# Hybrid conformer and sliding-window attention block on one Trainium2 core: value projection with features as rows, the queries' blocks in a buffer of their own, convolution taps behind each rotation

## The chip, the core and the metric

The kernel runs on one core of a Trainium2 chip. TensorE (PE in the profile, with its weight loads as PEld) multiplies, VectorE (DVE), ScalarE (ACT) and GpSimd (POOL) do the elementwise work, and SyncE (SP) issues the DMAs of the weights. The metric is device time in microseconds (us) of one execution; lower is better.

## The reference

One layer over 2048 tokens and 1024 features, in float32. Cut to what matters here:

```
u = rms_norm(h, g_pre_mix);  z = u @ w_in          # columns: GLU 2*512 | q 512 | k 128 | v 128 | gates 2*1024
a, b = split(z_glu);  c = a * sigmoid(b)
c = silu(layer_norm(causal_depthwise_conv(c, 31 taps)));  y_conv = c @ w_conv_out
q = apply_rope(q, 8 heads of 64);  k = apply_rope(k, 2 heads of 64);  v = 2 heads of 64
y_attn = sliding_window_sink_attention(q, k, v, sinks) @ w_attn_out   # chunks of 64, each sees itself and the one before
y = sig(gate_a) * y_conv + sig(gate_b) * y_attn;   h = h + rms_norm(y @ w_out)
u = rms_norm(h);  gate, val = split(u @ w_up);  gate = causal_depthwise_conv(gate, 3 taps)
h = h + rms_norm((gelu(gate) * val) @ w_down)
h = h + (p @ w_ple) * sigmoid(h @ w_ple_gate)
```

## The kernel before

**Tiling.** The 2048 tokens are worked off in four slices of T = 512 (`for c in range(CHUNKS)`). Inside a slice nearly every activation stands with its features on the 128 partitions and the 512 tokens along the row. Each float32 product is made of three: the stationary weight tile and the moving activations are split in a high and a low part (`w_hi`, `w_lo`, `u_hi`, `u_lo`), and `product` issues hi x hi, hi x lo and lo x hi. A block is eight 128 x 128 weight tiles; `full_block` runs its 24 matmuls of 512 columns into one PSUM bank. In the first slice a block arrives unsplit: ScalarE rounds it to `w_hi` (L356) and GpSimd subtracts (L318); in the others both parts are loaded.

**Order.** Each engine has its own program, written out by hand, and runs it strictly in that order; semaphores join them. In the mixing part of a slice TensorE computes the GLU blocks, then four query blocks and the key block (`B_QKV + j`, j = 0 to 4), the value block, then the attention, whose stages stand between the `gate_a` blocks, then the merge.

**Rotation.** For each of the five blocks ScalarE writes a copy with swapped halves into `rope_b` (four instructions, L409; `rope_b` has two buffers, so block j from 2 on waits until rotation j-2 is done), VectorE multiplies by cosine and sine and adds (L1101, L1102, then L1105 into `qT` for queries, or four times L1109 into `k_dup` for the keys). Every rotation counts up `rope_done`, so the keys' rotation is the fifth in a slice.

**Taps.** The 31-tap convolution is done by VectorE, one instruction for each tap and feature group (L1065 for tap 0, L1069 for the others). `early_taps(1, ...)` puts the 30 of the second half of the features ahead of the rotations: 8, 8, 8 and 6 of them ahead of rotations 0 to 3, none ahead of the keys'. Another 64 stand between the steps of the attention. After the last, VectorE sums the four groups (L1175), and TensorE turns that into a mean (`conv_mean`, L834), for which it waits in the middle of a `gate_b` block.

**Attention.** `attend_q` (ScalarE, L417 and L418) spreads two chunks' queries into the block-diagonal `q_diag`, which VectorE has zeroed (L1097). `scores(i)` is 24 small matmuls; `score_maxima` (VectorE), `attend_exp` (ScalarE), the normalisation (VectorE), a transpose (L794) and the product with the values (L802) follow. Between `scores(i)` and that transpose TensorE runs two `gate_a` blocks. `q_diag` shares its memory with part of `rope_b`, so `attend_q(0)` waits for all five rotations and for a new zeroing in every slice.

**Values.** Values are wanted with tokens on the partitions. So here the activations are the stationary side: L760 to L762 are 96 matmuls of 128 columns. ScalarE copies the bank into `v_even` and `v_odd` (L426 to L430) before the exponentials.

## Time and profile before

| what | us |
|---|---|
| median of 3 runs (lowest, highest) | 3052.93 (3051.05, 3054.32) |
| the profiled execution, its own time | 3054.54 |
| span in its trace | 3052.7 |
| PE busy | 2903.9 |
| DVE busy | 1564.0 |
| ACT busy | 920.4 |
| POOL busy | 299.7 |

The span runs from the first to the last instruction. Busy TensorE time counts overlapping matmuls once, and it says nothing about how wide they are. The chain that ended last is what set the time: at each step the work that released the next. The four slices begin at about 0, 827, 1566 and 2303 us of the span; the stretch that the change touches is about 60 to 250 us in the first and 890 to 1010 us in the second. The third and fourth have the timing of the second.

### The profile page before, as it was taken

The page shows a single profiled execution, that of the slowest core. Times are in us where ns is not written, and L with a number is a line of the kernel's source. Part 1 is how long each engine was busy: PE and PEld are TensorE (multiplying, and loading weights), DVE is VectorE, ACT ScalarE, POOL GpSimd, SP SyncE. Part 2 cuts the span into 40 slices and gives each one's busy share as a digit, 9 for nine tenths or more (in the row PEclk, how much of TensorE's full clock was granted, in tenths as well). Part 3 has the DMA queues.
Part 4 walks back from the last instruction along what each step waited for, and adds up shares of the span by engine and source line. Part 5 has one row for each costly group of instructions (what it writes and reads, how often), then busy time and mean ns, then how long its engine had stood idle before and what let it go on. Part 6 is the DMA issues. An engine that isn't in the chain of part 4 may idle for free.

```text
span 3052.7 us, 33514 instructions
## 1 busy us (share of the span) xinstructions
PE 2903.9 (95%) x13232; PEld 2401.6 (79%) x13232; DVE 1564.0 (51%) x2535; ACT 920.4 (30%) x1661; POOL 299.7 (10%) x126
## 2 busy tenths in 40 slices
PE   6888899999899999999999999999999999899998
PEld 5776778887788778888878887888887878788887
DVE  6894477325778426412458834540356862542035
ACT  3463343333426223111233522210123541311013
POOL 2223334444200000000000000000000000000000
PEclk8799999999999999999999999999999999999999
DMA  5445757877743454555454344455555345455555
GB/s 208 172 164 215 284 213 289 290 285 280 262 167 137 158 184 176 194 194 189 184 207 171 133 179 176 183 193 194 189 189 208 142 151 195 160 193 193 193 193 179
DMA packets 180925, 600.37 MB, mean 197 GB/s; under 512 B 18336, under 2 KB 37024, under 8 KB 180768
## 3 DMA queue, kind: packets, MB, share of 16 engines
q1 hardware_dynamic: 163872, 589.83, 53.0%
q10 hardware_dynamic: 16896, 8.39, 0.9%
q8 instruction: 105, 1.72, 0.2%
q14 instruction: 52, 0.43, 0.0%
HBM read 461.84 MB, written 136.31 MB: 196 GB/s over the span
## 4 chain that ended last, share of the span: by engine, by line
PE 79%; DVE 15%; ACT 3%; issue 2%; DMA 1%; POOL 0%; ACTq 0%; POOLq 0%; SPq 0%; DVEq 0%
PE ps L690 22%; PE ps L691 21%; PE ps L692 21%; DVE conv_acc L1069 7%; PE ps L711 4%; PE ps L712 4%; PE ps L715 4%; PE ps L731 1%; DVE prob L1151 1%; DVE s_max L1130 0%; POOL w_lo L318 0%; DVE ca_lo L1162 0%; DVE y_tmp L1205 0%; PE ps L724 0%; DVE h L1042 0%
## 5 line engine op out<-in xcount | busy, mean ns | idle before, releaser
L690 PE MATMUL ps<-y_hi,w_hi 128*128 128x512 f32 x1536 | 602.9, 392 | 7.8 <-POOL w_lo L318 5.2
L692 PE MATMUL ps<-y_hi,w_lo 128*128 128x512 f32 x1536 | 598.9, 390 | 0.0
L691 PE MATMUL ps<-y_lo,w_hi 128*128 128x512 f32 x1536 | 598.8, 390 | 0.0
L1069 DVE SCALAR_TENSOR_TENSOR conv_acc<-conv_in,col,conv_acc 128x512 f32<-128x512 f32 x480 | 350.9, 803 | 0.8
L318 POOL TENSOR_TENSOR w_lo<-w_stage,w_hi 128x1024 fp32r<-128x1024 f32 x122 | 299.5, 2456 | 515.5 <-ACT w_hi L356 515.5
L690 PEld LDWEIGHTS ps<-y_hi,w_hi 128*128 128x128 f32 x1536 | 289.1, 188 | 71.3 <-DVE f_val L1262 4.3
L692 PEld LDWEIGHTS ps<-y_hi,w_lo 128*128 128x128 f32 x1536 | 289.0, 188 | 60.6
L691 PEld LDWEIGHTS ps<-y_lo,w_hi 128*128 128x128 f32 x1536 | 289.2, 188 | 59.9 <-issue 1.0
L690 PE MATMUL ps<-u_hi,w_hi 128*128 128x512 f32 x800 | 320.9, 401 | 0.4 <-POOL w_lo L318 0.4
L691 PE MATMUL ps<-u_lo,w_hi 128*128 128x512 f32 x800 | 313.5, 392 | 0.0
L692 PE MATMUL ps<-u_hi,w_lo 128*128 128x512 f32 x800 | 313.4, 392 | 0.0
L690 PE MATMUL ps<-f_hi,w_hi 128*128 128x512 f32 x768 | 301.5, 393 | 2.2 <-DVE f_lo L1283 2.2
L691 PE MATMUL ps<-f_lo,w_hi 128*128 128x512 f32 x768 | 299.5, 390 | 0.0
L692 PE MATMUL ps<-f_hi,w_lo 128*128 128x512 f32 x768 | 299.5, 390 | 0.0
L356 ACT ACTIVATE w_hi<-w_stage 128x1024 fp32r<-128x1024 f32 x122 | 129.1, 1059 | 267.2 <-PE ps L692 214.4
L1293 DVE TENSOR_TENSOR f_lo<-ps,f_hi 128x512 fp32r<-128x512 f32 x8 | 5.2, 686 | 339.9 <-ACT f_hi L597 339.9
L690 PEld LDWEIGHTS ps<-u_hi,w_hi 128*128 128x128 f32 x800 | 152.0, 190 | 34.1 <-issue 3.4
L691 PEld LDWEIGHTS ps<-u_lo,w_hi 128*128 128x128 f32 x800 | 151.9, 190 | 33.5 <-issue 3.0
L692 PEld LDWEIGHTS ps<-u_hi,w_lo 128*128 128x128 f32 x800 | 151.5, 189 | 32.1
L711 PE MATMUL ps<-y_hi,w_hi 128*128 128x512 f32 x384 | 154.5, 402 | 17.8 <-ACT y_hi L548 9.9
L690 PEld LDWEIGHTS ps<-f_hi,w_hi 128*128 128x128 f32 x768 | 144.6, 188 | 33.4 <-DVE f_lo L1283 2.6
L691 PEld LDWEIGHTS ps<-f_lo,w_hi 128*128 128x128 f32 x768 | 144.5, 188 | 30.6 <-issue 1.0
(179 smaller groups left out, 3991.9 us busy)
## 6 DMA issues: line engine op xcount, KB each, us to landing
w_hi<-split_weights SPq DMA_DIRECT2D x366, 512.0 KB, 3.2
w_lo<-split_weights SPq DMA_DIRECT2D x366, 512.0 KB, 4.2
w_stage<-in_weights SPq DMA_DIRECT2D x122, 512.0 KB, 4.3
split_weights<-w_hi SPq DMA_DIRECT2D x122, 512.0 KB, 2.6
split_weights<-w_lo SPq DMA_DIRECT2D x122, 512.0 KB, 3.9
x_rows<-in_x SPq DMA_DIRECT2D x5, 2048.0 KB, 10.2
out_h<-ple ACTq DMA_DIRECT2D x32, 256.0 KB, 5.2
p_rows<-in_p SPq DMA_DIRECT2D x4, 512.0 KB, 5.9
```

The source lines that it names most:

```text
L318: nc.gpsimd.tensor_tensor(w_lo[:, b % SLOTS], w_stage[:, b % SLOTS], w_hi[:, b % SLOTS].bitcast(F32), ALU.subtract).then_inc(w_lo_ready, 1)
L356: copy(w_hi[:, b % SLOTS], w_stage[:, b % SLOTS], ACT.Copy).then_inc(w_hi_ready, 1)
L690: nc.tensor.matmul(bank, w_hi[:, slot, kk], hi, start=start, stop=False)
L691: nc.tensor.matmul(bank, w_hi[:, slot, kk], lo, start=False, stop=False)
L692: return nc.tensor.matmul(bank, w_lo[:, slot, kk], hi, start=False, stop=stop)
L711: nc.tensor.matmul(ps[:, banks[o]], w_hi[:, slot, first + o], hi[:, k], start=(k == 0), stop=False)
L712: nc.tensor.matmul(ps[:, banks[o]], w_lo[:, slot, first + o], hi[:, k], start=False, stop=False)
L715: last = nc.tensor.matmul(ps[:, banks[o]], w_hi[:, slot, first + o], lo[:, k], start=False, stop=(k == 7))
L731: nc.tensor.matmul(ps[:, BC], ones[:, :], diag[:, :, :].rearrange("p t n -> p (t n)"), start=True, stop=True).then_inc(bc_ready, 1)
L1069: V.scalar_tensor_tensor(dst, src, column("conv_w", t + j * TAPS), dst, ALU.mult, ALU.add).then_inc(conv_tap, 1)
L1151: V.tensor_tensor(prob[:, s], prob[:, s], s_rec[:, s].unsqueeze(2).broadcast_to([P, PAIRS, P]), ALU.mult).then_inc(pn_ready, 1)
L1293: V.tensor_tensor(f_lo[:, F1 - NP + k], ps[:, PV + k], f_hi[:, F1 - NP + k].bitcast(F32), ALU.subtract).then_inc(p_lo, 1)
```

## The change

It touches three engines, all in the stretch from the query blocks to the first scores.

1. The value block becomes a `full_block` like the others: 24 matmuls of 512 columns with features as rows, ScalarE copies the bank to `v_feat`, and `value_rows` on TensorE transposes it back into the same bank with four 128-column transposes. It stands behind `scores(0)`. ScalarE's copies into `v_even` and `v_odd` wait for them.
2. `q_diag` and `v_feat` get buffers of their own. `q_diag` is zeroed once, in the first slice, ahead of rotation 3.
3. ScalarE calls `attend_q(0)` ahead of the keys' swapped copies, as soon as four rotations are done; `scores(0)` waits for the fifth.
4. VectorE's early taps stand behind each rotation: 8, 8 and 8 behind rotations 0 to 2, none behind rotation 3, 6 behind the keys'.

```diff
-        q_diag = sb("q_diag", [P, 2, PAIRS, P], F32, at + 18 * K)
+        q_diag = sb("q_diag", [P, 2, PAIRS, P], F32)
+        v_feat = sb("v_feat", [P, T], F32)
...
@@ ScalarE
+                def attend_q(i):
+
+                    for s in range(2):
+                        now = ds(2 * CH * i + CH * s, CH)
+                        copy(q_diag[0:CH, s, :, 0:CH], qT[0:CH, :, now], ACT.Copy)
+                        copy(q_diag[CH:P, s, :, CH:P], qT[CH:P, :, now], ACT.Copy).then_inc(q_diag_ready, 1)
+
                 for j in range(PAIRS + 1):
                     split_block(B_QKV + j + 2)
+                    if j == PAIRS:
+                        act.wait_ge(rope_done, c * (PAIRS + 1) + PAIRS)
+                        act.wait_ge(q_zeroed, 1)
+                        attend_q(0)
                     done(B_QKV + j)
...
-                    if j >= 2:
+                    if 2 <= j < PAIRS:
                         act.wait_ge(rope_done, c * (PAIRS + 1) + j - 1)
...
-                act.wait_ge(rope_done, (c + 1) * (PAIRS + 1))
-                act.wait_ge(q_zeroed, c + 1)
-                attend_q(0)
                 split_block(B_GA + 1)
                 done(B_QKV + PAIRS + 1)
+                copy(v_feat[:, :], ps[:, V_BANK], ACT.Copy).then_inc(v_out, 1)
+                act.wait_ge(vt_done, c + 1)
                 v_new = four(ps[:, V_BANK])
@@ TensorE
-                ready(B_QKV + PAIRS + 1)
-                v_slot = (c * NB + B_QKV + PAIRS + 1) % SLOTS
-                for t in range(TT):
...
-                last.then_inc(block_done, 1)
+                full_block(B_QKV + PAIRS + 1, V_BANK, u_hi, u_lo)
                 pe.wait_ge(rope_done, c * (PAIRS + 1) + 4)
...
                 def scores(i):
                     for s in range(2):
                         pe.wait_ge(q_diag_ready, c * SUB + 2 * i + (s + 1))
+                        if i == 0 and s == 0:
+                            pe.wait_ge(rope_done, (c + 1) * (PAIRS + 1))
...
+                def value_rows():
+                    pe.wait_ge(v_out, c + 1)
+                    for t in range(TT):
+                        last = nc.tensor.transpose(ps[:, V_BANK, P * t:P * t + P], v_feat[:, P * t:P * t + P], ident[:, :])
+                    last.then_inc(vt_done, 1)
...
                 scores(0)
+                value_rows()
@@ VectorE
                 for j in range(PAIRS + 1):
-                    early_taps(1, min(EARLY, 4 * j), min(EARLY, 4 * j + 4))
-                    if j == PAIRS:
+                    if j == PAIRS - 1 and c == 0:
                         V.memset(q_diag[:, :, :, :], 0.0).then_inc(q_zeroed, 1)
...
                     dve.wait_ge(rope_done, c * (PAIRS + 1) + j + 1)
+                    if j < PAIRS - 1:
+                        early_taps(1, 4 * j, 4 * j + 4)
+                early_taps(1, 4 * (PAIRS - 1), EARLY)
```

On ScalarE, in the second slice, from the swapped copies of query block 2 to the first copy of the values, this stood in a row before (line numbers of the kernel before; L409 is the swapped copy, L417 and L418 are `attend_q(0)`):

```order
L409 ACTIVATE rope_b<-ps 32x512 [waits rope_done,block_done]
L409 ACTIVATE rope_b<-ps 32x512 x3
L409 ACTIVATE rope_b<-ps 32x512 [waits rope_done,block_done]
L409 ACTIVATE rope_b<-ps 32x512 x3
L409 ACTIVATE rope_b<-ps 32x512 [waits rope_done,block_done]
L409 ACTIVATE rope_b<-ps 32x512 x3
L417 ACTIVATE q_diag<-qT 64x4x64 [waits q_zeroed,rope_done]
L418 ACTIVATE q_diag<-qT 64x4x64
L417 ACTIVATE q_diag<-qT 64x4x64
L418 ACTIVATE q_diag<-qT 64x4x64
L426 ACTIVATE v_even<-v_even 64x128 [waits block_done]
```

and this stands there now (L421 is the swapped copy, L406 and L407 are `attend_q(0)`, L427 the copy to `v_feat`):

```order
L421 ACTIVATE rope_b<-ps 32x512 [waits rope_done,block_done]
L421 ACTIVATE rope_b<-ps 32x512 x3
L406 ACTIVATE q_diag<-qT 64x4x64 [waits q_zeroed,rope_done,block_done]
L407 ACTIVATE q_diag<-qT 64x4x64
L406 ACTIVATE q_diag<-qT 64x4x64
L407 ACTIVATE q_diag<-qT 64x4x64
L421 ACTIVATE rope_b<-ps 32x512 [waits block_done]
L421 ACTIVATE rope_b<-ps 32x512 x3
L427 ACTIVATE v_feat<-ps 128x512 [waits block_done]
L430 ACTIVATE v_even<-v_even 64x128 [waits vt_done]
```

The keys' four swapped copies moved from ahead of `attend_q(0)` to behind it, and the first of the values' copies waits for TensorE's transposes.

On VectorE, in the second slice, from the halo copy of the keys (L1092) to the second rotation, before:

```order
L1092 COPY k_dup<-k_dup 128x2x64 [waits trig_done]
L1065 TENSOR_SCALAR conv_acc<-conv_in,col 128x512 [waits k_halo]
L1065 TENSOR_SCALAR conv_acc<-conv_in,col 128x512
L1069 SCALAR_TENSOR_TENSOR conv_acc<-conv_in,col,conv_acc 128x512 [waits conv_tap] x6
L1101 TENSOR_TENSOR rope_a<-ps,cos_t 128x512 [waits rope_swapped,block_done]
L1102 TENSOR_TENSOR rope_b<-rope_b,sin_t 128x512
L1105 TENSOR_TENSOR qT<-rope_a,rope_b 128x512 [waits rope_step]
L1069 SCALAR_TENSOR_TENSOR conv_acc<-conv_in,col,conv_acc 128x512 [waits conv_tap,rope_done]
```

and now (L1097 is the halo copy, L1105, L1106 and L1109 are the rotation):

```order
L1097 COPY k_dup<-k_dup 128x2x64 [waits trig_done]
L1105 TENSOR_TENSOR rope_a<-ps,cos_t 128x512 [waits rope_swapped,block_done,k_halo]
L1106 TENSOR_TENSOR rope_b<-rope_b,sin_t 128x512
L1109 TENSOR_TENSOR qT<-rope_a,rope_b 128x512 [waits rope_step]
L1070 TENSOR_SCALAR conv_acc<-conv_in,col 128x512 [waits rope_done]
L1070 TENSOR_SCALAR conv_acc<-conv_in,col 128x512
L1074 SCALAR_TENSOR_TENSOR conv_acc<-conv_in,col,conv_acc 128x512 [waits conv_tap] x6
L1105 TENSOR_TENSOR rope_a<-ps,cos_t 128x512 [waits rope_swapped,block_done]
```

The first rotation moved ahead of the eight taps and stands next to the halo copy.

On VectorE, from the last taps ahead of rotation 3 to the first step of `score_maxima(0)` (L1127), before:

```order
L1069 SCALAR_TENSOR_TENSOR conv_acc<-conv_in,col,conv_acc 128x512 [waits conv_tap,rope_done]
L1069 SCALAR_TENSOR_TENSOR conv_acc<-conv_in,col,conv_acc 128x512 [waits conv_tap] x5
L1101 TENSOR_TENSOR rope_a<-ps,cos_t 128x512 [waits rope_swapped,block_done]
L1102 TENSOR_TENSOR rope_b<-rope_b,sin_t 128x512
L1105 TENSOR_TENSOR qT<-rope_a,rope_b 128x512 [waits rope_step]
L1097 MEMSET q_diag 128x1024 [waits rope_done]
L1101 TENSOR_TENSOR rope_a<-ps,cos_t 128x512 [waits rope_swapped,block_done]
L1102 TENSOR_TENSOR rope_b<-rope_b,sin_t 128x512
L1109 TENSOR_TENSOR k_dup<-rope_a,rope_b 64x512 [waits rope_step]
L1109 TENSOR_TENSOR k_dup<-rope_a,rope_b 64x512 x3
L1127 TENSOR_TENSOR ps<-ps,prev_bias 128x4x64 [waits qk_done,rope_done]
```

and now (L1113 is the keys' rotation into `k_dup`, L1134 the first step of `score_maxima(0)`):

```order
L1105 TENSOR_TENSOR rope_a<-ps,cos_t 128x512 [waits rope_swapped,block_done]
L1106 TENSOR_TENSOR rope_b<-rope_b,sin_t 128x512
L1109 TENSOR_TENSOR qT<-rope_a,rope_b 128x512 [waits rope_step]
L1105 TENSOR_TENSOR rope_a<-ps,cos_t 128x512 [waits rope_swapped,block_done,rope_done]
L1106 TENSOR_TENSOR rope_b<-rope_b,sin_t 128x512
L1113 TENSOR_TENSOR k_dup<-rope_a,rope_b 64x512 [waits rope_step]
L1113 TENSOR_TENSOR k_dup<-rope_a,rope_b 64x512 x3
L1074 SCALAR_TENSOR_TENSOR conv_acc<-conv_in,col,conv_acc 128x512 [waits conv_tap,rope_done]
L1074 SCALAR_TENSOR_TENSOR conv_acc<-conv_in,col,conv_acc 128x512 [waits conv_tap] x5
L1134 TENSOR_TENSOR ps<-ps,prev_bias 128x4x64 [waits qk_done]
```

The zeroing is gone, rotation 3 and the keys' rotation follow one another, and six taps stand between the keys' rotation and the maxima.

## Rows read from the trace of the kernel before

**Rows 1.** The page: the chain that ended last, shares of the span:

```profile
PE 79%; DVE 15%; ACT 3%; issue 2%; DMA 1%; POOL 0%; ACTq 0%; POOLq 0%; SPq 0%; DVEq 0%
```

**Rows 2.** VectorE's timeline, second slice: start us, us, engine, line, op, [idle, releaser]:

```profile
890.51 1.00 DVE L1065 TENSOR_SCALAR conv_acc<-conv_in,col 128x512 f32<-128x512 f32 x2
...
895.52 0.69 DVE L1101 TENSOR_TENSOR rope_a<-ps,cos_t 128x512 f32<-128x512 f32 x1
...
897.57 5.39 DVE L1069 SCALAR_TENSOR_TENSOR conv_acc<-conv_in,col,conv_acc 128x512 f32<-128x512 f32 x8
...
918.55 0.91 DVE L1097 MEMSET q_diag<- 128x1024 f32 x1 [0.28 <-DVE qT L1105]
...
920.64 2.79 DVE L1109 TENSOR_TENSOR k_dup<-rope_a,rope_b 64x512 f32<-64x512 f32 x4
927.17 0.43 DVE L1127 TENSOR_TENSOR ps<-ps,prev_bias 128x256 f32<-128x256 f32 x1 [3.74 <-PE ps L776]
```

**Rows 3.** ScalarE's timeline, same stretch:

```profile
893.02 2.40 ACT L409 ACTIVATE rope_b<-ps 32x512 f32<-32x512 f32 x4 [4.84 <-PE ps L692]
898.39 2.40 ACT L409 ACTIVATE rope_b<-ps 32x512 f32<-32x512 f32 x4 [2.97 <-PE ps L692]
...
923.46 0.42 ACT L417 ACTIVATE q_diag<-qT 64x256 f32<-64x256 f32 x1 [6.37 <-DVE k_dup L1109]
...
925.38 0.31 ACT L426 ACTIVATE v_even<-v_even 64x128 f32<-64x128 f32 x1 [0.21 <-PE ps L762]
...
928.89 1.28 ACT L436 ACT_TABLE_LOAD   x1 [1.37 <-DVE s_neg L1133]
```

**Rows 4.** Windows A:B: us, each engine's busy time (count), granted clock, DMA share, GB/s:

```profile
914.40:925.10 10.70, 10.70 (x97) 10.66 (x97) 8.63 (x13) 3.95 (x8) 0.00 (x0) 1.00 0.27 100
925.10:927.75 2.65, 2.65 (x26) 2.65 (x26) 0.50 (x3) 2.15 (x5) 0.00 (x0) 1.00 0.52 168
927.75:938.75 11.00, 11.00 (x51) 9.06 (x50) 8.03 (x21) 6.71 (x27) 0.00 (x0) 1.00 0.39 150
135.50:140.60 5.10, 5.08 (x24) 5.10 (x25) 1.21 (x4) 3.88 (x7) 2.36 (x1) 0.50 0.01 3
140.60:152.80 12.20, 12.20 (x50) 9.98 (x50) 9.57 (x19) 7.77 (x28) 2.50 (x1) 0.90 0.39 148
192.74:194.66 1.92, 1.92 (x9) 1.62 (x9) 1.85 (x5) 0.60 (x1) 0.00 (x0) 0.50 1.01 412
```

**Rows 5.** VectorE's timeline where it takes up the second scores:

```profile
941.56 0.69 DVE L1130 TENSOR_REDUCE s_max<-ps 128x4 f32<-128x512 f32 x1 [3.17 <-PE ps L776]
```

**Rows 6.** VectorE alone in one window: us, busy time (count), clock, DMA:

```profile
941.56:1002.46 60.90, 59.45 (x119) 1.00 0.36 130
```

**Rows 7.** PE's timeline at the convolution's mean, second slice:

```profile
1002.60 1.36 PE L834 MATMUL ps<-ssum,ones 128*128 128x512 f32 x2 [3.46 <-DVE ssum L1175]
```

**Rows 8.** Windows around idle stretches of PE, columns as in rows 4:

```profile
105.30:109.00 3.70, 0.00 (x0) 0.00 (x0) 3.70 (x6) 2.66 (x4) 0.91 (x1) 1.00 0.00 0
109.00:143.10 34.10, 28.32 (x126) 27.68 (x127) 27.57 (x42) 12.66 (x24) 6.77 (x3) 0.50 0.33 123
...
999.20:1002.60 3.40, 0.00 (x0) 0.03 (x1) 3.11 (x6) 0.00 (x0) 0.00 (x0) 1.00 0.34 136
1003.30:1006.70 3.40, 3.40 (x8) 2.31 (x7) 2.56 (x5) 1.23 (x2) 0.00 (x0) 0.50 0.00 0
```

**Rows 9.** First slice, VectorE's timeline:

```profile
95.46 3.09 DVE L1065 TENSOR_SCALAR conv_acc<-conv_in,col 128x512 f32<-128x512 f32 x2
...
104.48 7.47 DVE L1069 SCALAR_TENSOR_TENSOR conv_acc<-conv_in,col,conv_acc 128x512 f32<-128x512 f32 x8
```

**Rows 10.** First slice, ScalarE's timeline:

```profile
104.54 2.39 ACT L409 ACTIVATE rope_b<-ps 32x512 f32<-32x512 f32 x4 [9.03 <-DVE qT L1105]
...
134.54 0.42 ACT L417 ACTIVATE q_diag<-qT 64x256 f32<-64x256 f32 x1 [8.73 <-DVE k_dup L1109]
```

**Rows 11.** First slice, GpSimd's timeline:

```profile
108.09 2.65 POOL L318 TENSOR_TENSOR w_lo<-w_stage,w_hi 128x1024 fp32r<-128x1024 f32 x1 [9.83 <-ACT w_hi L356]
```

More of the change, by code:

```diff
@@ L243, in build_kernel @@
         glu_sig, glu_done, halo_in, conv_tap = map(sem, ("glu_sig", "glu_done", "halo_in", "conv_tap"))
-        rope_swapped, rope_step, rope_done, k_halo, v_step, v_ready = map(
-            sem, ("rope_swapped", "rope_step", "rope_done", "k_halo", "v_step", "v_ready"))
+        rope_swapped, rope_step, rope_done, k_halo, v_out, vt_done, v_step, v_ready = map(
+            sem, ("rope_swapped", "rope_step", "rope_done", "k_halo", "v_out", "vt_done", "v_step", "v_ready"))
         q_diag_ready, q_zeroed, v_cur_ready, qk_done, sm_step, sm_ready, exp_done, pn_ready, t_done, pt_ready, pv_done, \
```

10 lines of the change are left out of this document (removed).

## The prediction, written before the changed kernel ran

> **What bounds the kernel now.** I read the chain that ended last first: 79% of the span is TensorE, 15% VectorE [rows 1]. So I asked in which stretch VectorE is on the chain, and looked at the second slice engine by engine; the third and fourth repeat it to within 0.1 us. Three readings carry the argument.
>
> Until the second scores, TensorE sets the pace. Blocks follow each other without a gap, 5.44 us apart (ScalarE's swapped copies are released by them 5.4 us apart [rows 3]). The value block runs from 914.4 to 925.1 at full rate, the first scores follow at once to 927.75, and two `gate_a` blocks to 938.75 [rows 4]. VectorE waits for TensorE before both score maxima, 3.74 us and 3.17 us [rows 2, 5].
>
> From the second scores' maxima on, VectorE sets it. Between 941.56 and 1002.46 it works 59.45 of 60.90 us, and the rest lies between instructions [rows 6]. TensorE runs ahead of it, reaches the convolution's mean and stands 3.46 us until VectorE's last sum [rows 7]. So whatever moves the second scores moves the mean by the same amount, and all that stands behind it; an earlier end of TensorE's own work alone is worth nothing there.
>
> The keys' rotation is nearly late already: it ends at 923.43 (920.64 + 2.79 [rows 2]), `attend_q(0)` takes 1.70 us behind it (923.46 to 925.16 [rows 3]), and TensorE's value block ends at 925.1. The 10.7 us of the value block are what hides that chain.
>
> **The value block.** 96 matmuls of 128 columns take 10.7 us, 0.111 us each [rows 4]. 24 of 512 columns take the 5.44 us of any block. TensorE is done at 914.45 + 5.44 = 919.9, which is 5.2 us less work. The page "TensorE: Matmul & The Clock Gate" of the Trainium skill (section "Step-by-step: what each phase is for") says that throughput is purely the number of columns. By that rule 96 x 128 and 24 x 512 would cost the same and nothing would be saved; the row has 0.111 us for 128 columns against 0.227 us for 512, so here the trace speaks for a saving on the engine itself. The rule returns as a rival below.
>
> **What replaces the cover: VectorE's side, second slice.** Rotation 0 now comes first, but its swapped copy lands at 893.02 + 2.40 = 895.42 [rows 3], as before. The eight taps that filled this time (890.51 to 895.5 [rows 2]) are gone from there, so VectorE idles 5 us. Then: rotation 2.05 us (895.52 to 897.57 [rows 2]) to 897.5; taps, two of the first kind among them, 5.0 to 902.5; rotation 1 to 904.55; eight taps 5.3 (897.57, 5.39 with the overlap [rows 2]) to 909.9; rotation 2 to 911.9; taps to 917.2; rotation 3 to 919.25. Before it ended at 918.27, ahead of the zeroing [rows 2].
>
> **The added wait.** ScalarE now holds the keys' swapped copy behind `attend_q(0)`, and that waits for rotation 3. So: `attend_q(0)` 919.3 to 921.0 (1.70), swapped copy 2.40 to 923.45, keys' rotation 4.05 (919.38 to 923.43 before: the 918.55 zeroing ends, then 0.63, 0.68 and 2.79 [rows 2]) to 927.55. Queued behind the wait on ScalarE are the keys' copies and `v_feat`; VectorE idles 4.2 us for the former, TensorE for the rotation. The first scores start at 927.65 instead of 925.12: **+2.5 us**. The zeroing (0.91 us [rows 2]) is saved, but lies ahead of nothing that is waited for.
>
> **The transposes.** Four behind the scores. A 128-column matmul costs 0.111 us at full clock (the value block), so four cost 0.44; eight transposes at half clock took 1.92 us, so four take 0.96 there [rows 4]. The copy to `v_feat` (0.6 us, a quarter of the 2.40 of four copies of that width [rows 3]) ends near 924.1 and is hidden. On ScalarE the values' four copies (2.1 us, from 925.38 [rows 3]) move behind the transposes. VectorE has six taps (4.06 us) to do before the maxima, which it starts at about 931.6; the maxima are then ready at 933.3 and 934.4. From ScalarE's table load at 928.89 [rows 3] to the end of the normalisation at 934.3 (941.56 less 3.17 of idling and 4.06 of taps [rows 5]) lie 5.4 us. So the normalised values are there at 939, or at 942 if the transposes run late and at half clock; TensorE asks for them at 941.7, or at 945 in that case: hidden.
>
> **The clock.** TensorE has nothing between 919.9 and 927.65, 7.75 us. The trace before has 13 stretches of 3.3 to 11.7 us without TensorE work, and each was followed by the clock at half (1.2 of 2.4 GHz) or lay in it. The rows show two: after 105.3, and even after the 3.4 us at 999.2 the clock stood at 0.50 from 1003.3 to 1006.7 [rows 8]. And small matmuls did not bring it back: in the first slice it was low from 109.0 to 143.1 [rows 8] with 20.7 us of dense 128-column matmuls inside, and rose once `gate_a` had run for 2.5 us (windows 135.5 and 140.6 [rows 4]). So I take the clock as down when the scores start. Scores: 5.10 us instead of 2.65 [rows 4], +2.45. Transposes: +0.52. Two gate blocks: 12.2 against 11.0 in the first slice, +1.2; between +0.5 and +2.5 by where it rises; I take 1.3.
>
> **The sum.** Slices two to four: 2.5 + 0.44 + 2.45 + 0.52 + 1.3 = 7.2 us each, 21.7 together. It arrives in full at the second scores' maxima: VectorE's six taps (4.06 us) are over at about 946 and TensorE's scores come at 948.8.
>
> First slice. ScalarE's split of the value weights stood behind the swapped copy at 104.54, which waited 9.03 us for rotation 0 [rows 10]; GpSimd's half came at 108.09 [rows 11], so TensorE stood from 105.3 to 110.8 and ran the value block at half clock. Rotation 0 now starts at 95.46, so this wait goes, and the value block ends near 111. But TensorE then waits for the keys. I work VectorE's side: each GpSimd subtraction costs it about 2.1 us (eight taps 7.47 instead of 5.39; two first taps 3.09 instead of 1.00 [rows 2, 9]). 95.46 + four rotations 8.2 + 24 taps 15.6 + zeroing 0.9 + three collisions 6.2 = 126.4; `attend_q` and copy 4.2, keys 4.05, one more collision 2.1 (the next split now falls there): 136.8. Before, the scores started at 135.53, behind the first half of `attend_q(0)` at 134.54 [rows 10]. +1.3, and 0.96 for the transposes at half clock: **+2.2**, uncertain by 3 either way. Scores and gates were at half clock there already.
>
> Profiled execution: 3054.5 + 21.7 + 2.2 = 3078.4. It ran 1.6 us above the median of the runs shown, so in their terms **3077 us**, 24 us slower.
>
> **Rivals.**
> A. *The clock holds* over the stretch, or the stretch is shorter than I think because the wide value block saves less: TensorE then stands as little as 2.5 us, and only the late keys and the transposes are paid, 3 x 2.95 + 1 = 10 us slower: **3063**. Against it: the two prices of the value block, and rows 8. (The rule on columns of "TensorE: Matmul & The Clock Gate" in the Trainium skill would give this case, since the block would then still end at 925.1.)
> B. *The clock stays down through both gate blocks* in slices two to four: 11.0 becomes 22, +9.7 each instead of +1.3: **3102**. For it: 34 us in the first slice. Against it: there and at 1003 it rose with 512-column work.
> C. *The keys are not held.* If their swapped copy were ready when rotation 3 ends (the copy ran right behind its block before), their rotation would end at 923.3, scores 1.7 us earlier than now, less 0.44: -1.3 in three slices and about -4 in the first: **3045**. It decides from the point at which `attend_q(0)` is not on ScalarE ahead of the copy; the order of instructions has it ahead.
> D. *TensorE's work is what counts.* 3 x 4.8 us, and 5.5 + 20.7 - 5.4 - 0.4 = 20.4 in the first slice: **3018**. Against it: VectorE's share of the chain and the 3.46 us wait of rows 7.
> E. *Nothing is seen*: the holes fill each other, 3053.
>
> **How the numbers follow.** Forecast 0.72, A 0.12, B 0.05, C 0.06, D 0.03, E 0.02. A range of 3061 to 3089 holds the forecast with its uncertain terms (slices 2 to 4 by 1.2 up and 0.8 down each, the first by 3, and some more for how the rise of the clock falls) and most of A; it leaves out B, C, D and E. What a measurement tells from no change is 0.2%, 6 us. Faster: C and D, 0.09. Slower: forecast, B and most of A, 0.87. Within: E and the low edge of A, 0.04.
>
> **What would show it.** In the profile after, second slice: VectorE idle about 5 us ahead of rotation 0 and 4.2 us ahead of the keys' rotation; ScalarE's keys' copies starting some 1.7 us behind rotation 3; value block of 5.4 us; TensorE idle 7 to 8 us ahead of the first scores; scores of 5.1 us with the clock at 0.5; VectorE dense again from the second maxima to the mean, with TensorE waiting some 3.5 us there. The forecast is wrong if TensorE's gap is under 3 us, if the clock stays up over it, or if the keys' copy starts before `attend_q(0)` ends.

## The result

The changed kernel takes **3073.91 us** (median of 4 executions, 3072.04 to 3076.65) against 3053.62 us for the kernel before (4 executions, 3051.05 to 3055.86): ratio 1.0067, 95% interval 1.0050 to 1.0085, 20 us slower. The forecast was 3077 us, 24 slower. The profiled execution took 3072.47 us, with a span of 3070.6 us.

The page of the changed kernel, the chain that ended last by engine (before: [rows 1]):

```profile
PE 77%; DVE 16%; ACT 3%; issue 2%; DMA 1%; POOL 1%; ACTq 0%; SPq 0%; POOLq 0%; DVEq 0%
```

TensorE has lost two points of the chain; what it no longer does in the value block it waits instead. Where it waits is plain in the second slice. First VectorE's timeline of the changed kernel (start us, us, engine, line, operation, tiles, count, [idle before, releaser]), to be read against [rows 2]:

```profile
893.83 0.69 DVE L1105 TENSOR_TENSOR rope_a<-ps,cos_t 128x512 f32<-128x512 f32 x1 [5.08 <-ACT rope_b L421]
...
916.79 0.69 DVE L1109 TENSOR_TENSOR qT<-rope_a,rope_b 128x512 f32<-128x512 f32 x1
921.81 0.69 DVE L1105 TENSOR_TENSOR rope_a<-ps,cos_t 128x512 f32<-128x512 f32 x1 [4.33 <-ACT rope_b L421]
...
923.14 2.79 DVE L1113 TENSOR_TENSOR k_dup<-rope_a,rope_b 64x512 f32<-64x512 f32 x4
925.96 4.06 DVE L1074 SCALAR_TENSOR_TENSOR conv_acc<-conv_in,col,conv_acc 128x512 f32<-128x512 f32 x6
```

ScalarE's timeline over the same stretch (before: [rows 3]):

```profile
917.56 0.42 ACT L406 ACTIVATE q_diag<-qT 64x256 f32<-64x256 f32 x1 [7.63 <-issue]
...
919.29 2.39 ACT L421 ACTIVATE rope_b<-ps 32x512 f32<-32x512 f32 x4
921.71 0.60 ACT L427 ACTIVATE v_feat<-ps 128x512 f32<-128x512 f32 x1
932.42 0.31 ACT L430 ACTIVATE v_even<-v_even 64x128 f32<-64x128 f32 x1 [10.11 <-PE ps L784]
```

TensorE's timeline at the first scores and at the convolution's mean (before: [rows 7] for the mean):

```profile
926.07 0.66 PE L772 MATMUL ps<-k_dup,q_diag 128*128 128x64 f32 x2 [7.74 <-DVE k_dup L1113]
...
1007.18 0.67 PE L839 MATMUL ps<-ssum,ones 128*128 128x512 f32 x1 [3.44 <-DVE ssum L1182]
```

And the windows of the changed kernel (A:B, us, busy time and count of PE, PEld, DVE, ACT, POOL, granted clock, DMA share, GB/s), in the order value block, gap, first scores with transposes, two `gate_a` blocks, then the first slice's value block and gap (before: [rows 4]):

```profile
912.72:918.33 5.61, 5.61 (x25) 4.32 (x23) 4.73 (x8) 0.76 (x2) 0.00 (x0) 1.00 0.51 187
918.33:926.07 7.74, 0.00 (x1) 0.03 (x1) 4.14 (x7) 3.85 (x8) 0.00 (x0) 0.77 0.37 135
926.07:932.03 5.96, 5.96 (x28) 5.96 (x29) 5.81 (x13) 0.00 (x0) 0.00 (x0) 0.50 0.01 3
932.03:943.35 11.32, 11.32 (x51) 9.30 (x50) 5.94 (x16) 8.80 (x31) 0.00 (x0) 0.97 0.25 93
105.75:111.49 5.74, 5.74 (x24) 4.42 (x24) 5.67 (x9) 3.42 (x5) 0.87 (x1) 1.00 0.76 274
111.49:135.34 23.85, 0.00 (x1) 0.03 (x1) 19.19 (x24) 5.66 (x10) 4.24 (x2) 0.54 0.27 100
```

VectorE alone from the second maxima to the mean (before: [rows 6]):

```profile
945.90:1007.18 61.28, 59.43 (x119) 1.00 0.36 131
```

The reader is to see one chain. The value block is 5.2 us shorter: its 24 matmuls start 0.227 us apart, 5.45 us in all, where 96 started 0.111 us apart, 10.65 in all (the window's 5.61 us hold the last one to its end as well). Nothing follows it: `attend_q(0)` starts at 917.56, right behind the last step of rotation 3 (916.79 and 0.69 us; the profile names no releaser here), the keys' swapped copy starts at 919.29, when `attend_q(0)` is through, VectorE waits 4.33 us for it, and TensorE waits 7.74 us for the keys. The clock went to half at 922.45, inside the gap, and came back 10.24 us later, so scores and transposes ran at 0.50. From the second maxima on VectorE is dense again, and TensorE waits the same 3.4 us at the mean as before. The value block's start and the mean lie 94.46 us apart (912.72 to 1007.18), against 88.15 before (914.45 to 1002.60): **+6.3 us a slice**. The third and fourth slices repeat it: gaps of 7.75 and 7.76, half clock for 10.24 us each, and 744.0 us from mean to mean instead of 737.5.

### The profile page after: what moved, and what is told of

It is laid out like the page before. It is cut to its first block, busy times and chain, and to the rows that moved or that the text cites. A ratio compares the mean times of both kernels' runs of the same rounds, so it can differ in the third digit from the quotient of the medians.

```text
span 3070.6 us, 32963 instructions
## 1 busy us (share of the span) xinstructions
PE 2878.9 (94%) x12960; PEld 2374.8 (77%) x12960; DVE 1563.2 (51%) x2532; ACT 922.7 (30%) x1665; POOL 298.9 (10%) x126
## 4 chain that ended last, share of the span: by engine, by line
PE 77%; DVE 16%; ACT 3%; issue 2%; DMA 1%; POOL 1%; ACTq 0%; SPq 0%; POOLq 0%; DVEq 0%
PE ps L694 21%; PE ps L695 21%; PE ps L696 21%; DVE conv_acc L1074 7%; PE ps L715 3%; PE ps L716 3%; PE ps L719 3%; POOL w_lo L319 1%; PE ps L735 1%; DVE prob L1158 1%; DVE s_max L1137 0%; DMA w_stage<-in_weights 0%; DVE ca_lo L1169 0%; DVE y_tmp L1212 0%; PE ps L728 0%
## 5 line engine op out<-in xcount | busy, mean ns | idle before, releaser
L694 PE MATMUL ps<-u_hi,w_hi 128*128 128x512 f32 x832 | 333.5, 401 | 1.3 <-POOL w_lo L319 1.3
L695 PE MATMUL ps<-u_lo,w_hi 128*128 128x512 f32 x832 | 326.3, 392 | 0.0
L696 PE MATMUL ps<-u_hi,w_lo 128*128 128x512 f32 x832 | 326.1, 392 | 0.0
L695 PEld LDWEIGHTS ps<-u_lo,w_hi 128*128 128x128 f32 x832 | 158.3, 190 | 34.4 <-issue 2.6
L696 PEld LDWEIGHTS ps<-u_hi,w_lo 128*128 128x128 f32 x832 | 157.8, 190 | 33.6
```

The lines of the kernel that those rows point to most:

```text
L694: nc.tensor.matmul(bank, w_hi[:, slot, kk], hi, start=start, stop=False)
L695: nc.tensor.matmul(bank, w_hi[:, slot, kk], lo, start=False, stop=False)
L696: return nc.tensor.matmul(bank, w_lo[:, slot, kk], hi, start=False, stop=stop)
```

## The experiments

The whole set first. "Start" is the time from the start of the second slice's value block to the first scores, "gap" TensorE's idle time ahead of them, "low" how long the clock then stood at half (1.2 of 2.4 GHz), "rest" the time from the first scores' start to the convolution's mean, "first mean" when the first slice's mean is reached. All are from the profiled execution; times are medians. The third and fourth slices repeat the second, but for the low stretch of two kernels and one gap of the late taps' run, of which the last section tells.

| kernel | time, us | before beside it | ratio (95%) | start | gap | low | rest | first mean |
|---|---|---|---|---|---|---|---|---|
| before | - | - | - | 10.7 | 0.0 | 0 | 77.5 | 230.9 |
| after | 3073.91 | 3053.62 | 1.0067 (1.0050-1.0085) | 13.4 | 7.7 | 10.24 | 81.1 | 231.9 |
| value block alone | 3060.01 | 3052.75 | 1.0034 (1.0021-1.0046) | 10.0 | 4.4 | 6.83 | 80.9 | 232.5 |
| early queries alone | 3075.15 | 3051.66 | 1.0069 (1.0057-1.0081) | 12.4 | 1.6 | 3.41 | 79.1 | 236.5 |
| taps alone | 3049.54 | 3053.53 | 0.9984 (0.9975-0.9993) | 10.9 | 0.1 | 0 | 77.5 | 224.1 |
| after, keys first | 3052.68 | 3052.75 | 1.0004 (0.9995-1.0013) | 9.1 | 3.5 | 6.83 | 81.2 | 228.6 |
| after, taps ahead | 3079.04 | 3052.75 | 1.0089 (1.0075-1.0103) | 12.4 | 6.8 | 10.24 | 82.0 | 236.6 |
| after, narrow value block | 3071.13 | 3052.06 | 1.0063 (1.0049-1.0076) | 13.4 | 2.5 | 6.83 | 80.8 | 230.3 |
| after, gap filled | 3065.47 | 3052.75 | 1.0045 (1.0033-1.0058) | 13.4 | 0.5 | 0 | 77.9 | 232.8 |
| keys first, taps ahead | 3053.32 | 3052.06 | 1.0003 (0.9994-1.0012) | 8.1 | 2.5 | 3.41 | 79.6 | 234.1 |
| keys first, late taps | 3041.93 | 3052.06 | 0.9968 (0.9957-0.9980) | 7.0 | 1.4 | 0 | 78.8 | 223.3 |
| keys fourth | 3036.12 | 3052.06 | 0.9944 (0.9932-0.9957) | 5.8 | 0.2 | 0 | 77.9 | 228.2 |
| keys fourth, late taps in slice 1 | 3032.42 | 3053.53 | 0.9932 (0.9919-0.9944) | 5.8 | 0.2 | 0 | 78.0 | 224.4 |

### The keys' copy goes first again

The queries keep their own buffer; ScalarE only issues them behind the keys' swapped copy.

```
-                    if j == PAIRS:
-                        act.wait_ge(rope_done, c * (PAIRS + 1) + PAIRS)
-                        act.wait_ge(q_zeroed, 1)
-                        attend_q(0)
                     done(B_QKV + j)
...
-                    if 2 <= j < PAIRS:
+                    if j >= 2:
                         act.wait_ge(rope_done, c * (PAIRS + 1) + j - 1)
...
                     last.then_inc(rope_swapped, 1)
+                act.wait_ge(rope_done, c * (PAIRS + 1) + PAIRS)
+                act.wait_ge(q_zeroed, 1)
+                attend_q(0)
```

> The changed kernel with one thing put back: ScalarE copies the keys' swapped halves as soon as their block is done (it waits for rotation 2 only) and calls attend_q(0) behind that. Theory (the held copy is the main cause): the keys' rotation follows rotation 3 at once, VectorE's idle 4.3 us ahead of it goes, first scores 4.3 us earlier in each slice. TensorE's gap shrinks from 7.7 to about 3.5 us; whether the clock still falls over it is open, worth 3 us a slice at most. Time 3051 to 3061 us, against 3074 of the changed kernel. Rival (the order of the taps is the cause): the copy is cheap to hold, VectorE is late anyway, time stays above 3068. Rival (the transposes and the value block themselves): above 3068 too.

Measured: 3052.68 us, ratio 1.0004 (0.9995 to 1.0013). The order of two steps on ScalarE is worth the whole 21 us: between the profiled executions 14.3 us less from the value block to the mean in slices two to four together, and 3.3 less up to the first slice's mean. The timelines of ScalarE, VectorE and TensorE, second slice, columns as above:

```profile
906.87 2.40 ACT L417 ACTIVATE rope_b<-ps 32x512 f32<-32x512 f32 x4 [3.05 <-PE ps L695]
911.41 0.42 ACT L406 ACTIVATE q_diag<-qT 64x256 f32<-64x256 f32 x1 [2.15 <-DVE qT L1108]
```

```profile
904.06 5.39 DVE L1073 SCALAR_TENSOR_TENSOR conv_acc<-conv_in,col,conv_acc 128x512 f32<-128x512 f32 x8
909.37 0.69 DVE L1104 TENSOR_TENSOR rope_a<-ps,cos_t 128x512 f32<-128x512 f32 x1
...
911.41 0.69 DVE L1104 TENSOR_TENSOR rope_a<-ps,cos_t 128x512 f32<-128x512 f32 x1
...
912.74 2.79 DVE L1112 TENSOR_TENSOR k_dup<-rope_a,rope_b 64x512 f32<-64x512 f32 x4
```

```profile
915.67 0.41 PE L771 MATMUL ps<-k_dup,q_diag 128*128 128x64 f32 x2 [3.45 <-DVE k_dup L1112]
```

The copy now starts with the end of its block (906.87), VectorE runs the fourth rotation and the keys' back to back, and the keys' is done 8.9 us behind the value block's start instead of 13.2, 4.3 us sooner (the fourth stays at 4.8). But a gap of 3.45 us stays, and with it the low clock. It is VectorE's: eight taps from 904.06 to 909.4 stand between the third rotation and the fourth, whose copy had been there since 903.8.

### The taps go ahead of each rotation again

```
                 for j in range(PAIRS + 1):
+                    early_taps(1, min(EARLY, 4 * j), min(EARLY, 4 * j + 4))
...
-                    if j < PAIRS - 1:
-                        early_taps(1, 4 * j, 4 * j + 4)
-                early_taps(1, 4 * (PAIRS - 1), EARLY)
```

> The changed kernel with one thing put back: the early taps stand ahead of the rotations again (8, 8, 8, 6, none). Theory: rotation 3 ends only about 1 us earlier in slices 2 to 4, the keys' copy is still held, so the gap of TensorE is 6.7 us there and the clock still falls; in the first slice rotation 0 is late again, the value weights' split with it, and the keys' rotation some 3 us later than in the changed kernel. Time 3071 to 3077 us. Rival (taps are the main cause): near 3058 or below.

Measured: 3079.04 us, 5 us more than the changed kernel and 2 above the upper edge that was expected. In the second slice the scores start 0.9 us sooner, which the rest takes back (82.0 for 81.1); the loss is in the first slice, whose mean comes at 236.6 instead of 231.9. (The profiled execution took 3074.68 us, 4.4 below the median, so the rows hold only part of the 5 us.) So the place of the taps does not cause the slowdown; it softens it.

### Each part alone

The value block, `v_feat` and the transposes, in the kernel before:

```
-                ready(B_QKV + PAIRS + 1)
...
-                last.then_inc(block_done, 1)
+                full_block(B_QKV + PAIRS + 1, V_BANK, u_hi, u_lo)
...
                 scores(0)
+                value_rows()
```

> The kernel before with the value block alone changed: 24 wide matmuls, the copy with features as rows, four transposes behind the first scores; q_diag shared with rope_b and written behind the keys' rotation as before, taps as before. Theory: TensorE ends 5.2 us earlier but the first scores start when attend_q(0) has written its first half, 0.7 us earlier than before; a gap of about 4.5 us opens and the clock falls over it (about 3 us on scores, transposes and gates), 0.44 us of transposes: +2.7 us in each of slices 2 to 4, about +1 in the first, 3062 us (3058 to 3066). Rival (a saving on TensorE shows in the time): 3054 minus 15, 3039. Rival (the clock plays no part): 3053.

Measured: 3060.01 us. Its timelines of VectorE, ScalarE and TensorE, second slice:

```profile
915.13 0.91 DVE L1099 MEMSET q_diag<- 128x1024 f32 x1 [0.28 <-DVE qT L1107]
```

```profile
920.04 0.42 ACT L418 ACTIVATE q_diag<-qT 64x256 f32<-64x256 f32 x1 [6.37 <-DVE k_dup L1111]
```

```profile
921.02 0.66 PE L769 MATMUL ps<-k_dup,q_diag 128*128 128x64 f32 x2 [4.40 <-ACT q_diag L419]
```

The chain zeroing, keys, queries is as it was in [rows 2, 3]; only its cover has gone. TensorE's 5 us turn into 4.4 us of waiting, and the scores come a mere 0.7 us sooner; the low clock and the transposes cost 3.4 us behind them. A block that is 5 us shorter makes the kernel 7 us longer.

The queries' buffer and their early place, with narrow value block and taps as before:

```
-        q_diag = sb("q_diag", [P, 2, PAIRS, P], F32, at + 18 * K)
+        q_diag = sb("q_diag", [P, 2, PAIRS, P], F32)
...
+                    if j == PAIRS:
+                        act.wait_ge(rope_done, c * (PAIRS + 1) + PAIRS)
+                        act.wait_ge(q_zeroed, 1)
+                        attend_q(0)
...
```

> The second part of the change alone: the queries' blocks of the first two chunks have their own buffer and are written ahead of the keys' swapped copy; value projection of 96 narrow matmuls, no transposes, taps ahead of each rotation. The third rotation of the queries then ends behind 8 taps, the two copies of it hold the keys' swapped copy, and the scores start about as in the run with narrow block and taps behind (gap 2.5 us, half clock for 6.83 us in slices 2 to 4), while the first slice has the wait of 5.51 us ahead of the value block again. By that run (3071.1) and the 4 us between the two places of the taps: 3074 us, between 3070 and 3078. If the three parts simply added up (value block +7.3 us, taps -4.0, changed kernel +20.9), this one would have to be +17.6: 3071. If early queries cost nothing without the wide block, 3053.

Measured: 3075.15 us, 23.5 above the kernel before beside it. Its timelines of ScalarE and TensorE, second slice:

```profile
922.84 0.42 ACT L406 ACTIVATE q_diag<-qT 64x256 f32<-64x256 f32 x1 [6.69 <-issue]
...
924.58 2.39 ACT L421 ACTIVATE rope_b<-ps 32x512 f32<-32x512 f32 x4
```

```profile
931.35 0.41 PE L778 MATMUL ps<-k_dup,q_diag 128*128 128x64 f32 x2 [1.57 <-DVE k_dup L1119]
```

The held keys show here without any shorter block: the value block starts at 918.95 and the scores 12.4 us behind it instead of 10.7. The gap is only 1.57 us, but the clock falls behind it. From the value block to the mean that is 3.4, 5.0 and 5.0 us more in slices two to four, and the first slice's mean comes 5.7 us later, 19.1 of the spans' 21.2. This part alone is worse than the three together.

The taps behind each rotation, in the kernel before:

```
                 for j in range(PAIRS + 1):
-                    early_taps(1, min(EARLY, 4 * j), min(EARLY, 4 * j + 4))
...
                     dve.wait_ge(rope_done, c * (PAIRS + 1) + j + 1)
+                    if j < PAIRS - 1:
+                        early_taps(1, 4 * j, 4 * j + 4)
+                early_taps(1, 4 * (PAIRS - 1), EARLY)
```

> The third part of the change alone: the kernel before, with eight taps of the second pair behind each of the first three rotations instead of ahead of them and six behind the last; narrow value block, shared buffer, queries behind the keys. In slices 2 to 4 the keys are then ready about 8.9 us behind the value block's start, the clearing of the buffer takes 0.9 and the first copies of queries 0.85, which is 10.7 us against a block of 10.65: no gap worth naming, no change. In the first slice the value weights' split is queued on ScalarE behind a rotation that comes 5 us earlier, so that the wait of 5.51 us ahead of the value block falls to 1.3, and six taps (4.06 us) leave the way to the first scores: 1 to 5 us gained there. Sum: 3049 us, between 3046 and 3053. If the taps' place were what costs the changed kernel its 20 us, it would be above 3060.

Measured: 3049.54 us, 4 faster; the interval (0.9975 to 0.9993) lies below 1, though the gain is less than the 0.2% that the prediction took as its bound. ScalarE's and TensorE's timelines in the first slice of this kernel, against [rows 10]:

```profile
97.38 2.39 ACT L409 ACTIVATE rope_b<-ps 32x512 f32<-32x512 f32 x4 [3.85 <-DVE qT L1104]
99.80 1.06 ACT L356 ACTIVATE w_hi<-w_stage 128x1024 fp32r<-128x1024 f32 x1
```

```profile
104.58 0.33 PE L760 MATMUL ps<-w_hi,u_hi 128*128 128x128 f32 x1 [1.27 <-POOL w_lo L318]
```

The copy waits 3.85 us for the first rotation instead of 9.03, so the split of the value weights behind it leaves early enough, and the wait ahead of the value block is 1.27 us instead of 5.51. Every kernel of the table shows one of these two numbers (5.5 with the taps ahead of the rotations in the first slice, 1.3 with them behind), and the taps decide which.

The parts alone are worth +7.3, +23.5 and -4.0 us, 26.8 together; the whole change costs 20.3. They don't add up because two of them wait for the same thing: once the keys are held, a shorter value block delays little further. The next run bears that out: with both orders changed, the wide block adds 1.2 us (20.3 for 19.1, beside the kernel before), not 7.3. The taps keep their worth: behind the rotations they give 4.4 us with the queries early (19.1 for 23.5).

### The changed kernel with the narrow value block

```
-                full_block(B_QKV + PAIRS + 1, V_BANK, u_hi, u_lo)
+                for t in range(TT):
+                    tok = slice(P * t, P * t + P)
+                    for k in range(8):
...
-                value_rows()
```

> The changed kernel with the value projection as in the kernel before: 96 matmuls of 128 columns, no copy of the features and no transposes; both re-orderings stay. The held keys decide the start of the first scores, so these should stay where the changed kernel has them (13.4 us behind the value block's start) and the gap should shrink from 7.74 us to about 2.7, as the block is longer. If the cost of the change is the held keys and the clock that the long gap lets fall, this kernel wins the transposes (0.7 us a slice) and the half clock (about 3 us a slice): 3062 us, between 3060 and 3066. If the clock falls at the short gap as well, 3071. If the wide block by itself were what costs time, this kernel would be back at the kernel before, 3053.

Measured: 3071.13 us, on the value for a clock that falls at the short gap too. Its windows (value block, gap, scores):

```profile
912.95:923.78 10.83, 10.83 (x97) 10.69 (x95) 6.42 (x11) 4.01 (x8) 0.00 (x0) 1.00 0.28 98
923.78:926.30 2.52, 0.00 (x0) 0.03 (x1) 2.44 (x5) 2.09 (x4) 0.00 (x0) 1.00 0.57 176
926.30:930.80 4.50, 4.50 (x22) 4.50 (x23) 4.42 (x9) 0.00 (x0) 0.00 (x0) 0.53 0.33 135
```

The scores start 13.4 us behind the value block's start whether that block takes 5.6 us or 10.8 to its last matmul's end: the keys decide. And 2.52 us of gap were enough for half clock in the scores. I had expected the clock to hold at such a gap (3062 us); it did not.

### The gap filled

The changed kernel, with 32 matmuls of 512 columns whose result nobody reads between the value block and the first scores of slices two to four. This adds work and takes nothing from the scores' wait.

```
                 full_block(B_QKV + PAIRS + 1, V_BANK, u_hi, u_lo)
+                if c > 0:
+                    pe.wait_ge(glu_done, c * NC + 6)
+                    for _ in range(32):
+                        nc.tensor.matmul(ps[:, PV], y_hi[:, 0, 0:P], u_hi[:, 0], start=True, stop=True)
```

> The changed kernel with 32 matmuls of 512 columns on data that nothing reads, put between the value block and the first scores in slices 2 to 4 (7.3 us of the 7.7 us gap); everything else as changed. Theory: the first scores start when they did, but at full clock: scores 2.65 us instead of 5.25, transposes and gates 0.6 less, so 3.1 us less in each of three slices: 3065 us (3062 to 3067). The clock in the windows of the first scores is 1.00. Rival (the clock's fall costs nothing, since VectorE sets the pace behind it): 3074, the clock up all the same.

Measured: 3065.47 us, 8.4 below the changed kernel. Its windows over the later part of the value block with the filled gap, over the scores, and over the transposes:

```profile
918.50:929.70 11.20, 10.78 (x48) 8.60 (x46) 6.71 (x12) 4.62 (x9) 0.00 (x0) 1.00 0.45 168
929.79:932.60 2.81, 2.81 (x25) 2.81 (x26) 2.81 (x5) 0.00 (x0) 0.00 (x0) 1.00 0.00 0
932.60:933.30 0.70, 0.70 (x7) 0.65 (x6) 0.70 (x2) 0.12 (x1) 0.00 (x0) 1.00 0.00 0
```

The scores start where they did (13.4 us behind the value block's start), but at clock 1.00, and from their start to the mean it is 77.9 us instead of 81.1. From mean to mean the two later slices take 2.7 and 3.3 us less than in the changed kernel. So the clock's share is 3.2 us a slice, and the rest of the 6.3 is late keys (2.7) and transposes (0.4): before, that stretch had 77.5.

### Both orders back

Keys first and taps ahead, with the wide value block and the queries' own buffer.

> Both re-orderings at once: the keys' swapped copy goes back ahead of the first two chunks' queries, and the taps go back ahead of each rotation; the wide value block, its transposes and the queries' own buffer stay. If VectorE's order (8 taps between the third rotation and the fourth) is what still delays the keys by about 1 us in slices 2 to 4 (3.45 us of gap with the keys first, 2.5 by the count with the taps ahead), three slices give back 3 us; the first slice shows the other sign, since with the taps ahead alone the wait for the value weights was 5.51 us there and not 1.27. Sum: 3052.7 - 3 + 4 = 3054 us, between 3048 and 3058. The theory that the taps' place matters nowhere says 3052.7; the one that own buffer, early queries and early taps together bring the scores in with no wait would say below 3046.

Measured: 3053.32 us. The gap is the 2.5 us of the count, and the first slice's mean comes at 234.1 instead of 228.6. What slices two to four win (6.2 us together from the value block to the mean), the first one loses (5.4).

### Versions made from these reasons

Keys first, and the eight taps that delay the fourth rotation moved behind the first score maxima:

```
-                    if j < PAIRS - 1:
+                    if j < PAIRS - 2:
                         early_taps(1, 4 * j, 4 * j + 4)
-                early_taps(1, 4 * (PAIRS - 1), EARLY)
+                early_taps(1, 4 * (PAIRS - 2), EARLY - 4)
...
                 score_maxima(0)
+                early_taps(1, EARLY - 4, EARLY)
```

> The run with the keys first, with VectorE's last eight taps of the second pair (5.39 us, which lay between the third and the fourth rotation) moved behind the first score maxima, where VectorE waits 4.26 us for the exponentials. The fourth rotation and the keys' then follow their swapped copies at once: the keys are ready about 6.9 us behind the value block's start, the gap falls from 3.45 to 1.2 us. Three times 2.2 us and something in the first slice: 3045 us, between 3041 and 3049. If the rotation's place in VectorE's queue is not what the scores wait for, 3052.7; if the moved taps come to delay the softmax, above that.

Measured: 3041.93 us, 10.8 below the run with the keys first. TensorE's and VectorE's timelines, second slice:

```profile
916.39 0.41 PE L771 MATMUL ps<-k_dup,q_diag 128*128 128x64 f32 x2 [1.42 <-DVE k_dup L1112]
```

```profile
912.14 0.69 DVE L1104 TENSOR_TENSOR rope_a<-ps,cos_t 128x512 f32<-128x512 f32 x1 [3.30 <-ACT rope_b L417]
...
922.88 5.38 DVE L1073 SCALAR_TENSOR_TENSOR conv_acc<-conv_in,col,conv_acc 128x512 f32<-128x512 f32 x8
928.18 0.15 DVE L1155 TENSOR_TENSOR s_den<-s_den,s_sinke 128x4 f32<-128x4 f32 x1
```

VectorE waits for the keys' copy now (3.30 us) and no more for its own taps; the gap is 1.42 us and the clock stays up. The moved taps are a little too long for their new place: the normalisation starts right behind them at 928.18, without a wait, and the scores lie 78.8 us from the mean instead of 77.9. In the first slice the mean comes 5.3 us sooner. (The profiled execution took 3048.22 us, the other five 3040.62 to 3042.59; between the first mean and the second value block it took 686.1 us, the most of all the traces, which have 678.0 to 683.6 there.)

The keys' weights fourth in the stream, so that their rotation, the long one, is beside a block and not behind it; the first two chunks' queries behind the last rotation; taps ahead of the first three rotations from the second slice on:

```
-    for j in range(PAIRS + 2):
+    for j in (0, 1, 2, 4, 3, 5):
         column_of(w_in, first + j)
...
-                    if j < PAIRS:
+                    if j != KEYS_AT:
...
-                        act.wait_ge(rope_done, c * (PAIRS + 1) + PAIRS)
+                act.wait_ge(rope_done, (c + 1) * (PAIRS + 1))
```

> A version built on the reasons: the wide value block and the queries' own buffer stay, the keys' weights come fourth in the stream (first, second, third queries' block, keys, fourth queries' block, values), so that the keys' rotation, the long one of 4.2 us, lies beside the fourth queries' block; the queries of the first two chunks follow the last rotation; in slices 2 to 4 the taps lie ahead of the first three rotations, in the first slice behind them. By the rows of the run with the keys first: last swapped copy ends 2.7 us behind the value block's start, its rotation takes 2.1 us, two copies of queries 0.85, so the scores can start 5.7 us behind the start of a value block of 5.6 us: gap 0.1 to 0.9 us in place of 3.45. Three times 2.6 to 3.3 us, about 1 us a slice of clock that no longer falls, and 2 to 3 us in the first slice: 3040 us, between 3035 and 3046. If the first scores are not what sets a slice's end once the gap is under 3.5 us, it stays at 3052.

Measured: 3036.12 us, ratio 0.9944 (0.9932 to 0.9957). TensorE's timeline and the scores' window, second slice:

```profile
916.11 0.39 PE L696 MATMUL ps<-u_hi,w_lo 128*128 128x512 f32 x1
916.67 0.41 PE L772 MATMUL ps<-k_dup,q_diag 128*128 128x64 f32 x2 [0.17 <-issue]
```

```profile
916.67:919.58 2.91, 2.91 (x26) 2.91 (x27) 2.91 (x5) 1.35 (x3) 0.00 (x0) 1.00 0.67 221
```

The scores follow the value block at once and at full clock. Here most of the block's 5.2 us reaches the slice's end: 83.7 us from the value block's start to the mean, against 88.15 before and 94.5 after (85.8 with keys first and late taps, 87.7 with keys first and taps ahead).

The same with the late taps in the first slice alone:

```
...
                 score_maxima(0)
+                if c == 0:
+                    early_taps(1, EARLY - 4, EARLY)
```

> The version with the keys' weights fourth in the stream, with the late taps in the first slice only, where VectorE shares its time with GpSimd and its queue decides the start of the first scores: there eight taps (5.4 to 7.5 us) go behind the first score maxima. The two runs' first means stand at 228.22 us (keys fourth) and 223.29 us (late taps), slices 2 to 4 stay as with the keys fourth. Sum: 3036.1 - 4.5 = 3032 us, between 3029 and 3036. If the first slice's gain is taken back by the wait for the loads ahead of the second slice, 3036.

Measured: **3032.42 us**, ratio 0.9932 (0.9919 to 0.9944), 21 us faster than the kernel before and 41 faster than the changed one.

## Why the prediction was right, point by point

**What bounds the slice.** VectorE from the second maxima to the mean, so that a late start of the scores moves the mean by as much. In the table the rest stays at 77.5 us where the clock holds and there are no transposes, 77.9 with them, whether the scores start 5.8 or 13.4 us behind the value block's start; what is above that is the clock, or the late taps in their new place. TensorE's wait at the mean stayed at 3.4 to 3.5 us in all but the late taps' run (3.9). Right.

**The added wait.** Forecast: scores 2.5 us later, gap 7.75 us, VectorE idle 5 and 4.2 us. Measured: 13.35 us behind the value block's start instead of 10.67, so 2.7; gap 7.74; idle 5.08 and 4.33. Undone alone, the held copy gives 21 us back, the clock's part among them. Right.

**The value block.** Forecast 5.44 us, measured 5.45 from start to start (5.61 to the last one's end), against 10.65 for the same products in 128 columns. By the rule on columns of the Trainium skill ("TensorE: Matmul & The Clock Gate", section "Step-by-step: what each phase is for") both would take the same; by the rows here they don't. That the saving would be worth nothing was right in its reason: the run with the narrow block starts its scores at the same distance, 13.4 us.

**The clock.** That it would be down when the scores start was right, in all three slices. Its price was **mis-sized**: 2.45 + 0.52 + 1.3 = 4.3 us a slice in the forecast, 3.2 by the filled gap. Scores and transposes took 5.96 us, as forecast within 0.1 (5.10 + 0.96). The term that failed is the gates': 1.3 us, taken from the first slice, where they took 12.2 us. They took 11.32 against 11.00, so 0.3. The clock came back at 932.69, with the scores and transposes through and 0.7 us of the gates (932.03). In the first slice before, it had stayed down until 143.1, 2.5 us into the gates, after a much longer low stretch, and I had carried that tail over. Nor did the reading behind it hold, that small matmuls do not bring the clock back: in the changed kernel's first slice it came back at 140.79, when behind a gap of 23.85 us only scores and transposes had run, 0.26 us before the first gate matmul at 141.05. Windows over the scores with the transposes, before and after that moment:

```profile
135.34:140.79 5.45, 5.45 (x25) 5.45 (x26) 5.30 (x12) 0.00 (x0) 0.00 (x0) 0.50 0.12 44
140.79:141.05 0.26, 0.26 (x5) 0.26 (x4) 0.26 (x2) 0.00 (x0) 0.00 (x0) 0.99 0.00 0
```

The price follows from how long the clock stays low behind the start of the scores: 6.62 us here (926.07 to 932.69), of which half, 3.3 us, is what full clock would have saved.

**The transposes.** 0.44 us at full clock: the run with the filled gap has 77.9 in place of 77.5. Right. With that and the clock the rest is accounted for, so nothing waited for them or for the copy to `v_feat`.

**The sum.** Forecast 7.2 a slice; measured 6.3 in the second, from its value block on, and 6.3 and 6.7 from mean to mean in the others: 19.3 us for 21.7. First slice +2.2 forecast; its mean came 1.0 later (231.90 for 230.87), with rotation 0 at 94.65 instead of the 95.46 that I had started from. From there the way is 1.8 longer. The first scores did not come 1.3 us later but at 135.34 for 135.53: `attend_q(0)` started at 124.81, not at the 126.4 that I had added up. From the scores to the mean it is 1.2 us more, for 0.96. The filled-gap kernel has the same first slice and its mean at 232.79, so two executions of the same instructions differ here by 0.9 us, and a shift of 1.0 says little. The wait ahead of the value block did go (1.26 for 5.51), and the gap that took its place was 23.85 us. Between the first mean and the second value block the changed kernel's profiled execution gained 2.8 us that no term had. That is not the change: the filled-gap kernel runs the same instructions there and took 683.6 us, like the kernel before (683.6), where the changed kernel took 680.8. The clock was low there for 38.6 us in all before, for 34.1 with the gap filled and for 27.3 in the changed kernel. So the 2.8 us belong to the execution and not to the change. Of the spans' difference, 17.9 us, 1.0 - 2.8 + 19.3 = 17.6 (the fourth mean comes at 2495.27 for 2477.70) is there at the last mean.

**The rivals.** A (the clock holds) fell in the trace and, more sharply, with the narrow block: even the 2.5 us that it would have left bring half clock. B (down through both gate blocks) fell: 0.97 over them. Its sum was also short: 11.0 becoming 22 is +11 for the 1.3, three times 9.7 on top of 3077, so 3106 and not 3102. C is the run with the keys first: forecast 3045 there, measured 3052.68. Its start of the scores was right (9.1 us behind the value block's start for 10.7, 1.6 sooner where 1.7 was forecast); what the rival left out is the clock, which falls in the 3.45 us gap that a block of 5.6 us leaves, so that the rest takes 81.2 us. In the first slice it won 2.2 us, not 4. D needs the keys out of the way entirely: three times 4.8 us is what the version with the keys fourth comes near to (4.4 a slice); of its 20.4 us in the first slice that version won 2.7.

## What to carry to other kernels

When an edit shortens a block, ask first what that block was hiding; here it hid the keys' rotation, and 15 us of TensorE's work turned into 7 us of loss until the keys were moved. In an engine's queue the cheap copy that is needed first must not stand behind one that waits for something later: that order on ScalarE was worth 21 us, more than anything that the change saved. And work that may lie anywhere (the taps) is best put where its engine waits; its place was worth 4 us alone and 11 us once it stood between the last two rotations.

## What the runs showed of the hardware that I had not expected

The clock fell behind gaps as short as 1.57 us, and the length of the gap decided neither whether it fell nor for how long. In the second slice it was low for 10.24 us behind a gap of 7.74, for 6.83 us behind 3.45 and behind 2.52 (narrow block), but for 3.41 us behind 2.51 (keys first, taps ahead) and behind 1.57 (early queries alone). It did not fall at 0.17 or 1.42, nor at 1.78 in the third slice of the run with the late taps.

The same gap in the same kernel, with the same work around it, gave different lengths. With early queries alone the gaps of slices two to four are 1.57, 1.59 and 1.57 us and the clock is low for 3.41, 6.83 and 6.83 us. With keys first they are 3.45, 3.46 and 3.45 us, and it is low for 6.83, 3.41 and 6.83. So the two cases at 2.5 us need no cause in the width of the matmuls ahead of them, and what does decide stays open.

What a low stretch costs can be read: near half of the part that lies behind the scores' start. Above the rest of 77.9 us with transposes (77.5 without), 3.41 us cost 1.6 to 1.7 (79.6, and 79.1 without), 6.62 us of the changed kernel's 10.24 cost 3.2, 6.83 us cost 3.3 (81.2, and 80.8 without), and 8.45 us with the taps ahead cost 4.1 (82.0). Whoever shortens a gap without closing it may win nothing on the clock: from 7.74 to 3.45 us of gap the rest stayed at 81.1 and 81.2 us.
